# The last gate bias put into PSUM ahead of its products, and the last sum of squares begun from the earlier mean

## The reference

```python
def rmsnorm(x, g):
    xf = x.astype(jnp.float32)
    y = xf * lax.rsqrt(jnp.mean(xf * xf, axis=-1, keepdims=True) + EPS)
    return (y * g.astype(jnp.float32)).astype(x.dtype)
...
        gte = jax.nn.sigmoid(rmsnorm(h, g_ple[i]) @ w_pgate[i] + b_pgate[i])
        h = h + (p[i] @ w_ple[i]) * gte
    return rmsnorm(h, g_final)
```

## Time and profile before

| | |
|---|---|
| median of 3 runs | 1161.87 us (1161.85 to 1162.01) |
| the profiled execution | 1161.71 us |
| its span, from first to last instruction | 1159.9 us |
| PE, busy share of the span | 99% |
| DVE, ACT, POOL | 78%, 61%, 11% |
| mean granted clock of PE | 0.998 |
| stores at the end | 7 issues on two queues |

### The profile page before, as it was taken

The page is one execution under the profiler, slowest core; times in us unless marked ns, Lnnn a source line. Parts: engine busy times, 40 slices in busy tenths (PEclk is TensorE's granted clock), DMA queues, the critical chain, the costliest instruction groups (busy, mean ns, idle before and its releaser), DMA issues.

```text
span 1159.9 us, 16445 instructions
## 1 busy us (share of the span) xinstructions
PE 1147.7 (99%) x5618; PEld 968.7 (84%) x5618; DVE 899.9 (78%) x1192; ACT 709.7 (61%) x969; POOL 125.2 (11%) x74
## 2 busy tenths in 40 slices
PE   9999999999999999999999999999999999999996
PEld 8889989988888878888888888888888888888886
DVE  6589767767777998978888887888787888837674
ACT  6544465466455676766758566667667575757552
POOL 0212443436031000000000000000000000000111
PEclk9999999999999999999999999999999999999999
DMA  9655555454555566564746474755647475754541
GB/s 343 216 183 180 182 182 167 161 179 148 200 167 178 181 240 205 199 225 146 252 146 239 160 252 145 253 176 193 209 157 243 144 252 161 238 212 154 200 160 73
DMA packets 113120, 223.38 MB, mean 193 GB/s; under 512 B 5193, under 2 KB 6417, under 8 KB 112816
## 3 DMA queue, kind: packets, MB, share of 16 engines
q1 hardware_dynamic: 112608, 222.08, 56.8%
q10 hardware_dynamic: 464, 0.66, 0.2%
HBM read 220.63 MB, written 2.10 MB: 192 GB/s over the span
## 4 chain that ended last, share of the span: by engine, by line
PE 92%; DVE 2%; ACT 2%; issue 2%; POOL 1%; POOLq 0%; DVEq 0%; ACTq 0%
PE ps L1655 11%; PE ps L1657 11%; PE ps L1656 11%; PE ps L1452 8%; PE ps L1454 8%; PE ps L1453 8%; PE ps L1439 6%; PE ps L1441 6%; PE ps L1440 6%; PE ps L1486 3%; PE ps L1485 3%; PE ps L1484 3%; PE ps L1494 2%; PE ps L1648 1%; PE ps L1649 1%
## 5 line engine op out<-in xcount | busy, mean ns | idle before, releaser
L655 ACT ACTIVATE w_hi<-w_raw 128x1024 fp32r<-128x1024 f32 (+1 forms) x286 | 290.8, 1026 | 218.0 <-PE ps L1454 120.1
L978 DVE TENSOR_TENSOR w_lo<-w_raw,w_hi 128x1024 fp32r<-128x1024 f32 x250 | 301.4, 1218 | 142.8 <-ACT w_hi L655 142.5
L1452 PE MATMUL ps<-w_hi,nT_hi 128*128 128x512 f32 x280 | 111.4, 398 | 0.0
L1454 PE MATMUL ps<-w_hi,nT_lo 128*128 128x512 f32 x280 | 109.1, 390 | 0.0
L1453 PE MATMUL ps<-w_lo,nT_hi 128*128 128x512 f32 x280 | 109.0, 389 | 0.0
L579 POOL TENSOR_TENSOR w_lo<-w_raw,w_hi 128x1024 fp32r<-128x1024 f32 x36 | 86.7, 2409 | 181.7 <-ACT w_hi L655 181.7
L978 DVE TENSOR_TENSOR w_extra<-w_raw,w_extra 128x1024 fp32r<-128x1024 f32 (+1 forms) x60 | 67.1, 1132 | 37.6 <-ACT w_extra L655 35.4
L1034 DVE SCALAR_TENSOR_TENSOR ps<-arena,taps,ps 128x256 f32<-128x256 f32 x232 | 94.7, 483 | 0.2 <-ACT ps L776 0.2
L1655 PE MATMUL ps<-w_hi,nT_hi 128*128 128x512 f32 x220 | 86.5, 393 | 0.0
L1657 PE MATMUL ps<-w_hi,nT_lo 128*128 128x512 f32 x220 | 85.8, 390 | 0.0
L1656 PE MATMUL ps<-w_lo,nT_hi 128*128 128x512 f32 x220 | 85.6, 389 | 0.0
(11 more groups left out here) (285 smaller groups left out, 2823.6 us busy)
## 6 DMA issues: line engine op xcount, KB each, us to landing
w_raw<-in_w_gate SPq DMA_DIRECT2D x88, 512.0 KB, 4.0
w_raw<-in_w_up SPq DMA_DIRECT2D x88, 512.0 KB, 4.8
w_raw<-in_w_down SPq DMA_DIRECT2D x44, 1024.0 KB, 5.0
w_raw<-in_w_in SPq DMA_DIRECT2D x32, 1024.0 KB, 5.1
w_raw<-in_w_out SPq DMA_DIRECT2D x16, 1024.0 KB, 5.0
w_raw<-in_w_pgate SPq DMA_DIRECT2D x16, 1024.0 KB, 5.0
w_raw<-in_w_in SPq DMA_DIRECT2D x14, 512.0 KB, 10.7
w_raw<-in_w_ple SPq DMA_DIRECT2D x2, 1024.0 KB, 7.0
```

The source lines that it names most:

```text
L655: nc.scalar.activation(tiles_of(m)[0], source_of(m), ACT.Copy).then_inc(hi_ready, 1)
L978: nc.vector.tensor_tensor(lo, source_of(m), hi.bitcast(F32), ALU.subtract).then_inc(lo_ready, 1)
L1452: nc.tensor.matmul(banks[t][:, :], x_hi[:, k, rows], hi[:, k], start=start, stop=False)
L1454: ins = nc.tensor.matmul(banks[t][:, :], x_lo[:, k, rows], hi[:, k], start=False, stop=stop)
```

## The change

1. A new tile `inv_rstd` of two columns, allocated behind `power`. POOL fills it with `msq * rstd`, which is 1 over `rstd`, right after the root it already makes for this norm.
2. ACT copies the bias of the last 512 columns, times `inv_rstd`, into the banks of the three pieces. It does so in its list ahead of the splits of halves `LAST + 4` and `LAST + 5`, after waits for `inv_rstd`, for the rows of the bias and for `gate_in` 4.
3. PE waits for one seed per piece in place of `gate_in` 4, and its first matmul into each bank no longer starts the sum.
4. The sigmoid of the pieces waits for PE and reads PSUM, with `rstd` as its scale; DVE's logits of the pieces are gone.
5. The last sum of squares takes the mean of the other columns as its initial value and signals POOL itself; the addition behind it is gone, with its wait.

```diff
@@ tiles and semaphores
         power = sb("power", [P, TT])
+        inv_rstd = sb("inv_rstd", [P, TT])
         warm = sb("warm", [P, TT])
...
+        inv_ready, bias_seeded = sem("inv_ready"), sem("bias_seeded")
...
@@ POOL
             root(2, 3)
+            pool.wait_ge(rstd_ready, 4)
+            nc.gpsimd.tensor_tensor(inv_rstd[:, :], msq[:, 2], rstd[:, 2], ALU.mult).then_inc(inv_ready, 1)
             pool.wait_ge(rows_loaded, 32)
@@ ACT
+            def seed_bias():
+
+                sc.wait_ge(inv_ready, 1)
+                sc.wait_ge(rows_loaded, 32)
+                sc.wait_ge(gate_in, 4)
+                for i, (t, cols) in enumerate(LAST_PIECES):
+                    b_cols = slice(3 * NP + cols.start, 3 * NP + cols.stop)
+                    nc.scalar.activation(last_banks[i][:, cols], b_rows[:, b_cols], ACT.Copy, scale=inv_rstd[:, t:t + 1]).then_inc(bias_seeded, 1)
...
+                if m == LAST - 2:
+                    seed_bias()
                 for i in splits_at(m):
                     split_hi(i)
             for i, (t, cols) in enumerate(LAST_PIECES):
-                sc.wait_ge(gate_in, 6 + i + 1)
-                nc.scalar.activation(gate_p[:, t, cols], gate_p[:, t, cols], ACT.Sigmoid).then_inc(gate_p_ready, 1)
+                sc.wait_ge(last_done, i + 1)
+                nc.scalar.activation(gate_p[:, t, cols], last_banks[i][:, cols], ACT.Sigmoid, scale=rstd[:, 2, t:t + 1]).then_inc(gate_p_ready, 1)
@@ DVE
-                ve.wait_ge(last_done, i + 1)
-                gate_logits(3, t, cols, last_banks[i][:, cols])
                 last_gated(i)
...
-                nc.vector.tensor_tensor_reduce(out=gate_p[:, t, cols], in0=h[:, t, h_cols], in1=h[:, t, h_cols], scale=1.0 / D, scalar=0.0,
-                                               op0=ALU.mult, op1=ALU.add, accum_out=late[:, t:t + 1]).then_inc(late_mean, 1)
-                ve.wait_ge(late_mean, t + 1)
                 ve.wait_ge(early_mean, t + 1)
-                nc.vector.tensor_tensor(late[:, t:t + 1], late[:, t:t + 1], msq[:, 3, t:t + 1], ALU.add).then_inc(msq_ready, 1)
+                nc.vector.tensor_tensor_reduce(out=gate_p[:, t, cols], in0=h[:, t, h_cols], in1=h[:, t, h_cols], scale=1.0 / D,
+                                               scalar=msq[:, 3, t:t + 1], op0=ALU.mult, op1=ALU.add, accum_out=late[:, t:t + 1]).then_inc(msq_ready, 1)
@@ PE
-            pe.wait_ge(gate_in, 4)
             for i, (t, cols) in enumerate(LAST_PIECES):
+                pe.wait_ge(bias_seeded, i + 1)
...
-                        nc.tensor.matmul(dst, nT_hi[:, row, tok], hi[:, k, cols], start=row == 0, stop=False)
+                        nc.tensor.matmul(dst, nT_hi[:, row, tok], hi[:, k, cols], start=False, stop=False, skip_group_check=True)
```

More of the change, by code:

```diff
@@ L414, in hybrid_decoder_layer @@
         y_gain_ready, y_vector_ready, y_scalar_ready = sem("y_gain_ready"), sem("y_vector_ready"), sem("y_scalar_ready")
-        early_sum, early_mean, late_mean, last_rstd = sem("early_sum"), sem("early_mean"), sem("late_mean"), sem("last_rstd")
+        inv_ready, bias_seeded = sem("inv_ready"), sem("bias_seeded")
+        early_sum, early_mean, last_rstd = sem("early_sum"), sem("early_mean"), sem("last_rstd")
         block = ctx.enter_context(nc.Block())
@@ L1820, in _ @@
                         dst, tok = last_banks[i][:, cols], slice(t * P, (t + 1) * P)
-                        nc.tensor.matmul(dst, nT_hi[:, row, tok], hi[:, k, cols], start=row == 0, stop=False)
-                        nc.tensor.matmul(dst, nT_hi[:, row, tok], lo[:, k, cols], start=False, stop=False)
-                        ins = nc.tensor.matmul(dst, nT_lo[:, row, tok], hi[:, k, cols], start=False, stop=row == KC - 1)
+                        nc.tensor.matmul(dst, nT_hi[:, row, tok], hi[:, k, cols], start=False, stop=False, skip_group_check=True)
+                        nc.tensor.matmul(dst, nT_hi[:, row, tok], lo[:, k, cols], start=False, stop=False, skip_group_check=True)
+                        ins = nc.tensor.matmul(dst, nT_lo[:, row, tok], hi[:, k, cols], start=False, stop=row == KC - 1, skip_group_check=True)
                 ins.then_inc(last_done, 1)
```

## The result

The changed kernel takes 1167.47 us (median of 6 runs, 1166.91 to 1168.01), the kernel before in the same rounds 1161.86 (6 runs, 1161.31 to 1162.32): a ratio of 1.0048, with an interval from 1.0037 to 1.0059. It is slower by 5.6 us, and outside the predicted range of 1160.9 to 1162.3. The profiled execution took 1166.91 us for a span of 1165.1, with a mean granted clock of 0.998, as before.

What follows compares the result with a forecast made beforehand. PE, busy 99% of the span, bounds the kernel, with some nine microseconds of small chained steps behind its end. Gains of 0.41 and 0.14, the rest zero, took 1161.87 to 1161.3 us; range 1160.9 to 1162.3.

Steps and rivals of the forecast that it cites:

- Edit 4: `inv_rstd` moves `w_extra`, `w_more`, `a_last` and the arena to odd multiples of 32 bytes; taken at zero.
- slower, by this address: Rival: matmuls in PE's loop slow by 3.5 ns on 1,020, 3.6 us, giving 1164.9; chance 0.07.
- Edit 1: End of the kernel: DVE's logits step goes, the sigmoid reads PSUM with a row scale; 0.41 us gained.
- Edit 2: Last mean: the reduction starts from the earlier mean, the addition goes; 0.14 us gained, 0.06 pointer cost included.
- Edit 3: Last panel: three ACT seed copies of bias into PSUM, 1.62 us, covered before PE needs them; taken at zero.
- the 0.55: Total forecast gain at the kernel's end, 0.41 + 0.14 us off 1161.87.

Runs made afterwards that it cites:

- everything moved: Kernel before with a 32-byte pad ahead of `w_raw`, the first tile, so every tile moves by 32 bytes; 1161.90 us, ratio 1.0001.
- the period: Kernel before with the halves of `w_extra` as own tiles at +128 and +192 bytes, `w_more`, `a_last` and arena at +256; 1166.77 us.
- all edits, pad widened: Changed kernel with the unused tile ahead of `w_extra` at 256 bytes in place of 32; 1161.35 us, ratio 0.9996.
- small distances: Kernel before with the halves of `w_extra` at +16 and +48 bytes, `w_more`, `a_last` and arena at +64; 1169.59 us.
- both moved: Kernel before with `w_extra` moved by 32 bytes and `w_more`, `a_last` and arena by 64; 1168.02 us.
- after: The changed kernel with all its edits, against the kernel before; 1167.47 us, ratio 1.0048.
- which pair: Kernel before with a pad behind `w_extra`, which keeps its place, while `w_more`, `a_last` and arena move by 32 bytes; 1166.77 us.
- back on the grid: Changed kernel with the unused tile ahead of `w_extra` 32 bytes larger, so `w_extra`, `w_more`, `a_last` and arena start at 64-byte multiples; 1165.21 us, ratio 1.0028.

## Why the prediction was wrong

**Edit 4, the address, is the step that failed.** It said: "I take zero, from DVE's row". That row is of another engine, and of its own reads; it could not bear on a matmul, in which PE streams one operand while it takes in the block for the next. The rival "slower, by this address" had the right place (the loop), sign and test (PE's end, then the spacing of the matmuls on `w_extra`), but the wrong size and form. It priced one address at 3.5 ns on 1,020 matmuls. Measured are 6.6 and 7.0 ns on 778 of them, nothing on the 230 whose two operands moved together, and 1.3 us on those behind: 5.84 us in all against 3.6. It decided the sign from 0.5 ns a matmul and passed the 0.2% from 2.8, and the trace had no row of PE off its usual places to set against that; 0.07 was too small a chance for such a term on an engine that is busy 99% of the span.

The code held a sign that the prediction does not mention. The pad `align` was there, unused: with it the small tiles ahead of `w_extra` add up to a whole multiple of 512 bytes, and the trace before showed a median spacing of 226 to 227 ns for every pair of 512-column operands. The prediction reckoned from 64-byte multiples. The Trainium skill (SBUF — State Buffer, Operand start alignment) asks for a start at a multiple of the element size, and says that its own runs timed nothing. The runs here move 4-byte elements by multiples of 16 bytes, all within that rule, and lie between 1161.9 and 1169.6 us for one and the same computation.

**Edit 1** was taken at 0.41 and gave 0.46. The sigmoid took 0.47, as the PSUM row with a pointer said; the Trainium skill (ScalarE: Activation LUTs, What ACT_TABLE_LOAD costs) gave an estimated 492 ns, 20 more than measured. ACT took up PE's result after 0.03 to 0.04, not the 0.09 of the weight split in the earlier trace rows; why these differ was not tested.

**Edit 2** was taken at 0.14 and gave 0.13: the pointer costs 0.06 on the reduction (0.48 against 0.42 in the earlier trace rows), and the root starts 0.08 behind the end of the accumulator's read, as forecast.

**Edit 3** was taken at nothing and cost nothing: 1.48 us of seeds against 1.62, covered by 4.4 us. POOL's product took 1.21 us where the prediction had 0.7, hidden too.

**The sum** without edit 4 was 1161.3. With the tiles at a free distance the runs show 1161.41 and 1161.35. That total alone can't bear out the 0.55, since neither ratio excludes no change; the tail read in the profiles, 0.59 shorter, does. So of the forecast's terms only the address was far off.

**Open.** The runs say when PE is slow, not why. Distance modulo 256 does not give the size of the cost either: 64 bytes above `oT` and `nT` cost 2.2 and 4.3 ns for two tiles, 64 below `a_last` cost 6.0. Whether the sign of the distance makes that difference, or the tiles do, was not separated, nor what the 236 ns ahead of `a_last` are. That 256 is free, and so the period, rests on one offset in two kernels. Distances above 256 other than multiples of 512 were not tried, nor other widths and types.

## What to carry to other kernels

Where PE is the bound, treat any new or resized tile that lies ahead of PE's operands as an edit to every matmul on them, with a price of its own. Compare the starts of the streamed tile and of the stationary one modulo 256 bytes before and after, put small tiles behind the large ones or give them the slot of a pad (the second was tried here), and look at the distance between successive starts for each pair. A cost for which the trace has no row on the engine in question gets bounds from a measurement, or a wide range; a row of another engine is not evidence that it is zero.

## What the runs showed of the hardware

PE's distance between matmuls of 512 fp32r columns depends on where the streamed tile starts against the stationary one that is loaded meanwhile (means over the whole run; a distance is given without its sign, but 64 above and 64 below apart):

| distance in bytes | mean distance of starts | from |
|---|---|---|
| 0, all at their old places | 226.67 ns | the kernel before |
| 0, all moved by 32 | 226.7 | everything moved |
| 256 | 226.67 | the period; all edits, pad widened |
| 16 | 232.2 and 233.4 | small distances |
| 32 | 233.1 to 233.7 (232.3 for `w_extra` past `oT` in both moved) | after; which pair; both moved |
| 48 | 232.8 and 234.8 | small distances |
| 64, streamed tile above | 228.8 and 231.0 | back on the grid |
| 64, streamed tile below `a_last` | 232.6 | the period |
| 128 and 192 | 232.3 to 232.7 | the period |

A group of such matmuls also slows the six to eight behind it, whose own operands are at a free distance. POOL took 1.21 us for a product of 128 by 2 elements, and 0.70 for a power of the same size. ACT started 0.03 us after PE's last matmul, where a split of weights had waited 0.09.
